# Two transformer blocks in fp32 on one core: weight rings and tiles at multiples of 128 bytes, stationary weights written 72 or 80 bytes further on

## The reference, cut to what matters

```python
# first block
h = rmsnorm(x, attn_norm_w)
proj = h @ w_in                      # attention q, k, v; gated linear attention q, k, v, gate, low-rank codes
x = x + concat([attention, gla]) @ w_out
h = rmsnorm(x, ffn_norm_w)
x = x + (silu(h @ w_gate) * (h @ w_up)) @ w_down
x = rmsnorm(x, final_norm_w)
# second block, modulated by mod = silu(c) @ w_ada + b_ada
h = rms_norm(x, norm_mix) * (1 + sc1) + sh1
x = x + g1 * (hybrid_mixer(h @ w_in_2) @ w_out_2)      # retention, RWKV-7, block-sparse attention
h = rms_norm(x, norm_ffn) * (1 + sc2) + sh2
u = causal_depthwise_conv3(h @ w_ffn_up) + conv_b
x = x + g2 * ((silu(gate) * val) @ w_ffn_down)
out = rms_norm(x, norm_final)
```

## The kernel before, in words

| stage, line | form | matmuls |
|---|---|---|
| mixer 1, L574: q0, k0, q1, k1, gq, gk, 8 units each | columns | 1,152 |
| mixer 1, L574: v0, v1, gv0, gv1, gr0, gr1 (8 units each), out (8 parts of 4) | rows | 576 + 384 |
| mixer 1, L558: codes, 32 weight columns stationary | columns | 48 |
| GLU and conv, each: L574 (2 blocks of 8 units) and L306 (20 blocks) | columns | 384 and 3,840 |
| down 1 and down 2, each: L1762 | rows | 960 |
| down 1 and down 2, each: L1779, the last units, half of them from the ring | rows | 48 + 48 |
| mixer 2, L2084: 9 parts of 8 units | columns | 1,728 |
| mixer 2, L2084 and L2360: 4 parts of 8 units, out (8 parts of 4) | rows | 720 and 48 |

## Time and profile before

### The profile page before, as it was taken

How to read it: one execution, slowest core, us unless ns; L and a number is a source line. 1 busy time by engine, 2 the same in 40 slices (tenths; PEclk the granted TensorE clock), 3 DMA queues, 4 the chain that set the end, 5 groups by cost and what they waited for, 6 DMA issues and landing times.

```text
span 2445.8 us, 43133 instructions
## 1 busy us (share of the span) xinstructions
PE 2425.4 (99%) x18001; PEld 2205.9 (90%) x18001; DVE 1621.5 (66%) x1962; ACT 1149.9 (47%) x1516; POOL 0.3 (0%) x5
## 2 busy tenths in 40 slices
PE   9999999999999999999999999999999999999998
PEld 8889778999999998888899898988999999998886
DVE  5568457777777766777777455566878756664456
ACT  5465344534334334444664344445544444554444
POOL 0000000000000000000000000000000000000000
PEclk9999999999999999999999999999999999999999
DMA  8555467778777766888476344455677655555553
GB/s 280 171 170 182 150 225 268 268 263 289 275 265 285 272 238 251 317 312 293 154 279 242 125 142 139 139 185 195 245 271 258 224 207 189 190 203 193 188 187 121
DMA packets 214566, 541.27 MB, mean 221 GB/s; under 512 B 9130, under 2 KB 15860, under 8 KB 202516
## 3 DMA queue, kind: packets, MB, share of 16 engines
q1 hardware_dynamic: 214420, 539.18, 63.0%
HBM read 533.86 MB, written 5.28 MB: 220 GB/s over the span
## 4 chain that ended last, share of the span: by engine, by line
PE 97%; DVE 1%; ACT 1%; DMA 0%; issue 0%; SPq 0%; DVEq 0%; ACTq 0%
PE ps L306 36%; PE ps L1762 18%; PE ps L574 18%; PE ps L2084 15%; PE ps L1779 2%; PE ps L2602 0%; DMA raw_weights<-in_w_in_dram 0%; PE ps L2360 0%; PE ps L2621 0%; PE ps L974 0%; PE ps L1004 0%; PE ps L432 0%; PE ps L2616 0%; PE ps L986 0%; PE ps L1016 0%
## 5 line engine op out<-in xcount | busy, mean ns | idle before, releaser
L272 DVE TENSOR_TENSOR weights_lo<-raw_weights,weights_hi 128x1024 fp32r<-128x1024 f32 x786 | 957.9, 1224 | 745.4 <-ACT weights_hi L265 741.5
L265 ACT ACTIVATE weights_hi<-raw_weights 128x1024 fp32r<-128x1024 f32 x782 | 827.0, 1061 | 1182.0 <-PE ps L306 459.2
L485 DVE SCALAR_TENSOR_TENSOR ada_acc<-ada_w,col,ada_acc 128x1024 f32<-128x1024 f32 x180 | 230.1, 1278 | 0.1
L306 PE MATMUL ps<-glu_x_hi,weights_hi 128*128 128x256 f32 x1280 | 202.8, 280 | 0.0
L306 PE MATMUL ps<-glu_x_lo,weights_hi 128*128 128x256 f32 x1280 | 202.5, 279 | 0.0
L306 PE MATMUL ps<-glu_x_hi,weights_lo 128*128 128x256 f32 x1280 | 202.5, 279 | 0.0
L306 PE MATMUL ps<-conv_x_hi,weights_hi 128*128 128x256 f32 x1280 | 198.8, 277 | 0.0
L306 PE MATMUL ps<-conv_x_hi,weights_lo 128*128 128x256 f32 x1280 | 197.9, 277 | 0.0
L306 PE MATMUL ps<-conv_x_lo,weights_hi 128*128 128x256 f32 x1280 | 197.9, 277 | 0.0
L306 PEld LDWEIGHTS ps<-glu_x_lo,weights_hi 128*128 128x128 f32 x1280 | 173.2, 188 | 0.0
L306 PEld LDWEIGHTS ps<-glu_x_hi,weights_hi 128*128 128x128 f32 x1280 | 173.1, 188 | 0.0
(11 more groups left out here) (531 smaller groups left out, 3688.2 us busy)
## 6 DMA issues: line engine op xcount, KB each, us to landing
raw_weights<-in_w_in_dram SPq DMA_DIRECT2D x99, 1024.0 KB, 5.3
ada_w<-in_w_ada_dram SPq DMA_DIRECT2D x96, 1024.0 KB, 6.9
raw_weights<-in_w_ffn_up_dram SPq DMA_DIRECT2D x88, 1024.0 KB, 5.3
raw_weights<-in_w_gate_dram SPq DMA_DIRECT2D x44, 1024.0 KB, 5.1
raw_weights<-in_w_up_dram SPq DMA_DIRECT2D x44, 1024.0 KB, 5.1
raw_weights<-in_w_down_dram SPq DMA_DIRECT2D x44, 1024.0 KB, 5.4
raw_weights<-in_w_ffn_down_dram SPq DMA_DIRECT2D x44, 1024.0 KB, 4.8
raw_weights<-in_w_out_dram SPq DMA_DIRECT2D x32, 1024.0 KB, 5.1
```

What stands on the lines that cost most here:

```text
L265: kit.nc.scalar.activation(kit.w_hi_t[:, n % SPLITS, :], raw, ACT.Copy).then_inc(kit.w_hi, 1)
L272: kit.nc.vector.tensor_tensor(kit.w_lo_t[:, n % SPLITS, :], raw, kit.w_hi_t[:, n % SPLITS, :].bitcast(F32), ALU.subtract).then_inc(kit.w_l ...
L306: ins = nc.tensor.matmul(out, lhsT=lhsT, rhs=rhs, start=start and m == 0, stop=(k == KT - 1 and m == 2), skip_group_check=True)
L485: step = nc.vector.scalar_tensor_tensor(acc, w, c, acc, ALU.mult, ALU.add)
```

## The change

1. `weights_hi` and `weights_lo` get 32 values (128 bytes) more in each of the four slots, so a slot starts 4,224 bytes after the one before instead of 4,096, still at a multiple of 128.
2. `base` is rounded up to a multiple of 128 instead of 32. The rings have grown by 1,024 bytes, so it goes from 110,784 to 111,872 = 874 x 128: all tiles that stood at 64 modulo 128 now stand at 0.
3. `Kit.move` records ranges of units that are written further on in their slot: 80 bytes for the columns parts of mixer 1 and for the GLU, 72 bytes for the columns parts of mixer 2 and for conv. The rows parts and both down stages stay at the slot's start. `Kit.slots` gives a unit's two places, and the splits and the matmuls use it instead of `w_hi_t[:, n % SPLITS, :]`. (The codes part is moved too.)

Modulo 128, before and after: columns form, weights at 0 and x at 64, then weights at 80 or 72 and x at 0. Rows form, x at 64 and weights at 0, then both at 0. The last four units of a down stage: x and weights both at 64, then both at 0. The number, order, shape and waits of all instructions and transfers stay.

```diff
@@
+LINE = 128
+MOVED = {"m1": 80, "glu": 80, "m2": 72, "conv": 72}
@@ class Kit
-        self.w_hi_t = sb("weights_hi", [P, SPLITS, UNIT], dt=R32)
-        self.w_lo_t = sb("weights_lo", [P, SPLITS, UNIT], dt=R32)
+        self.w_hi_t = sb("weights_hi", [P, SPLITS, UNIT + LINE // 4], dt=R32)
+        self.w_lo_t = sb("weights_lo", [P, SPLITS, UNIT + LINE // 4], dt=R32)
+        self.moved = []
@@
+    def move(self, first, units, stage):
+
+        self.moved.append((first, first + units, MOVED[stage] // 4))
+
+    def slots(self, n, i=0):
+
+        u = n + 16 * i if isinstance(i, int) else n
+        at = sum(by for a, b, by in self.moved if a <= u < b)
+        return tuple(w[:, n % SPLITS, at:at + UNIT] for w in (self.w_hi_t, self.w_lo_t))
+
@@ split_hi
-    kit.nc.scalar.activation(kit.w_hi_t[:, n % SPLITS, :], raw, ACT.Copy).then_inc(kit.w_hi, 1)
+    kit.nc.scalar.activation(kit.slots(n, i)[0], raw, ACT.Copy).then_inc(kit.w_hi, 1)
@@ split_lo
-    kit.nc.vector.tensor_tensor(kit.w_lo_t[:, n % SPLITS, :], raw, kit.w_hi_t[:, n % SPLITS, :].bitcast(F32),
-                                ALU.subtract).then_inc(kit.w_lo, 1)
+    hi, lo = kit.slots(n, i)
+    kit.nc.vector.tensor_tensor(lo, raw, hi.bitcast(F32), ALU.subtract).then_inc(kit.w_lo, 1)
@@ multiply_block, and in the same way multiply_part, multiply_tiles, Down.tensor, Down.slot, last_units
-        s = n % SPLITS
+        w_hi, w_lo = kit.slots(n, i)
...
-                        wh, wl = (w[:, s, a + c0:a + c1] for w in (kit.w_hi_t, kit.w_lo_t))
+                        wh, wl = (w[:, a + c0:a + c1] for w in (w_hi, w_lo))
@@ FirstMixer
+            if p.form != "rows":
+                kit.move(n, p.units, "m1")
@@ Glu
+        kit.move(self.first, 16 * self.turns, "glu")
@@ SecondMixer
+            if p.form != "rows":
+                kit.move(self.first + n, p.units, "m2")
@@ ConvGlu
+        kit.move(self.first, 16 * self.turns, "conv")
@@ program
-        base = -(-nc.sbuf_base // 32) * 32
+        base = -(-nc.sbuf_base // LINE) * LINE
```

More of the change, by code:

```diff
@@ L294, in multiply_block @@
                         out = kit.ps[:, 2 * j + q, :]
-                        wh, wl = (w[:, s, a:a + UN] for w in (kit.w_hi_t, kit.w_lo_t))
+                        wh, wl = (w[:, a:a + UN] for w in (w_hi, w_lo))
                         h, l = (x[:, k, q * P:(q + 1) * P] for x in (xh, xl))
@@ L542, in multiply_part @@
 def multiply_part(kit, pe, part, n, u, x_hi, x_lo, begun=None):
-    nc, j, s = kit.nc, part.j, n % SPLITS
+    nc, j = kit.nc, part.j
+    w_hi, w_lo = kit.slots(n)
     per = UNIT // part.width
@@ L554, in multiply_part @@
         if part.form == "codes":
-            wh, wl = (w[:, s, a + P - 2 * GRANK:a + P] for w in (kit.w_hi_t, kit.w_lo_t))
+            wh, wl = (w[:, a + P - 2 * GRANK:a + P] for w in (w_hi, w_lo))
             h, l = x_hi[:, k, :], x_lo[:, k, :]
@@ L569, in multiply_part @@
                 out = kit.ps[:, 2 * j + q // 2, (q % 2) * S:(q % 2 + 1) * S]
-                wh, wl = (w[:, s, a + q * P:a + (q + 1) * P] for w in (kit.w_hi_t, kit.w_lo_t))
+                wh, wl = (w[:, a + q * P:a + (q + 1) * P] for w in (w_hi, w_lo))
                 h, l = x_hi[:, k, :], x_lo[:, k, :]
@@ L871, in half_hi @@
         act.wait_ge(self.s_whalf[c], 16)
-        self.kit.nc.scalar.activation(self.kit.w_hi_t[:, 2 * c, :], raw_half(self.kit, 2 * c), ACT.Copy
+        self.kit.nc.scalar.activation(self.kit.slots(2 * c)[0], raw_half(self.kit, 2 * c), ACT.Copy
                                       ).then_inc(self.kit.w_hi, 1)
@@ L1759, in unit @@
                     for q in range(2):
-                        wh, wl = (x[:, s, q * UN:(q + 1) * UN] for x in (kit.w_hi_t, kit.w_lo_t))
+                        wh, wl = (x[:, q * UN:(q + 1) * UN] for x in (w_hi, w_lo))
                         lhsT, rhs = ((h, wh), (h, wl), (l, wh))[m]
@@ L1800, in slot @@
             return tuple(w[:, x, :] for w in self.ext)
-        s = (self.first + p) % SPLITS
-        return self.kit.w_hi_t[:, s, :], self.kit.w_lo_t[:, s, :]
+        return self.kit.slots(self.first + p)
     def tail_hi(self, act, p):
@@ L1820, in next_hi @@
         act.wait_ge(kit.weights_used, self.first + 2 * self.w_tiles - 4)
-        kit.nc.scalar.activation(kit.w_hi_t[:, n % SPLITS, :], raw_half(kit, n), ACT.Copy).then_inc(kit.w_hi, 1)
+        kit.nc.scalar.activation(kit.slots(n)[0], raw_half(kit, n), ACT.Copy).then_inc(kit.w_hi, 1)
     def tail_lo(self, dve, p):
@@ L2352, in last_units @@
     def last_units(self, p, u, hi, lo, t):
-        kit, s = self.kit, (self.first + p.start + u) % SPLITS
+        kit = self.kit
+        w_hi, w_lo = kit.slots(self.first + p.start + u)
         for kk in range(2):
-            wh, wl = (w[:, s, kk * UN:(kk + 1) * UN] for w in (kit.w_hi_t, kit.w_lo_t))
+            wh, wl = (w[:, kk * UN:(kk + 1) * UN] for w in (w_hi, w_lo))
             h, l = (x[:, t * P:(t + 1) * P] for x in (hi[kk], lo[kk]))
```

## The result

The changed kernel takes 2454.51 us (median of 4 runs, 2454.23 to 2456.48) against 2443.67 before (2441.71 to 2445.43): ratio 1.0048, interval 1.0033 to 1.0062, 10.8 us slower. I had forecast 2388, and the range ended at 2436. The profiled spans are 2453.0 and 2445.8, so the profiles show 7.2 of these us. A span is 1.6 us shorter than the time of the same execution (2453.0 for 2454.56), so before's profiled execution took about 2447.4 us by estimate, 3.7 above its median; that is the rest.

What follows compares the result with a forecast made beforehand. It took the spacing of TensorE's matmul starts to bound the kernel. Rows form −25.0, columns form −34.1 and mixer waits +3.4 made −55.7 us, from 2443.6 to a forecast of 2388 us, range 2340 to 2436.

Steps and rivals of the forecast that it cites:

- I take the floor: Columns form, all stages: the new distances keep every matmul at 113.3 ns; 7,658 matmuls gain 4.45 ns each, −34.1 us.
- bound (+16): Columns form: +16 us if the new distance puts the other 3,670 matmuls at 117.8 ns.
- 85%: Mixers: share of their 2,880 columns-form matmuls taken to stand at 117.8 ns, 2,450 with something to gain.
- The rows form: Ring matmuls with x stationary: 3,744 go from 233.3 to 226.7 ns, −25.0 us.
- The distance is now that of the down_last units: Rows form: ring and x both at 0 modulo 128 give the 226.7 ns seen at the down stages' ends.
- rival 3: Rows form: period longer than 128 bytes, slots at 0 or 128 by 256; half the gain goes, 2400, chance 0.06.
- 113.3 is a floor: Columns form: 113.3 ns is the least for a 256-column matmul, since 32-column codes loads run no faster.
- The +3.4 us for waits in the mixers: Mixers: 15% of their 22.4 us gain counted as given back to waits for other engines, +3.4 us.
- Writes 72 or 80 bytes on: ScalarE's and VectorE's splits: shifted writes cost 0; 16 us for 786 splits at 20 ns without cover.
- The rule that the prediction set against its rows: TensorE: independent read ports, so addresses could not matter and time stays 2443.6; the rows say 25 us less.
- 2: Columns form: new distance worse, unaligned loads touch more memory; slower from 118.5 ns, 2511 at 124.5, chance 0.14.
- 1: Columns form: ignores 80 or 72, keeps its mix of spacings, 2420, chance 0.17; all at 117.8 ns, 2436, chance 0.07.

Runs made afterwards that it cites:

- The sweep: Columns-form weights at other distances from x modulo 256, a different one per stage, otherwise as e1; six kernels, 2438.59 to 2456.37 us.
- e1: Against the changed kernel: slots 4,352 bytes apart, base 128 past a multiple of 256, no offsets, so distance 0 modulo 256 everywhere; 2464.71 us, ratio 1.0091.
- e2: As e1, but with the change's offsets kept (80 in mixer 1 and GLU, 72 in mixer 2 and conv); 2449.66 us, ratio 1.0026.
- e9: As e1, but columns-form weights at distance 208 in all four stages, rows form at 0; 2429.05 us, ratio 0.9942.
- e14: As e10, but L306's matmuls in GLU and conv load and write 32 of 128 weight columns, GLU at distance 0; 2439.04 us.
- e10: As e1, but columns-form weights at distance 192 (that of the kernel before) in all four stages, rows form at 0; 2437.64 us, ratio 0.9973.

## Why the prediction was wrong

**The step that failed is the columns form's: "I take the floor".** It was −34.1 us in the sum and measured about +20 in the changed kernel: conv +16.3, mixer 2 some +2.7 and mixer 1 +1.0 (start-to-start means 118.1 for 116.6 and 117.7 for 116.9, over 1,728 and 1,152 matmuls), GLU 0. I had no row for 80 or 72, and argued that a shift of a few bytes loosens a lock. The sweep shows the reverse: among the distances tried the 113.3 exists at 64 and 192 alone, before's 192 was one of them, and every other one gives 116.6 or more. A third of the columns matmuls already stood at 113.3, and I priced their loss only as a bound (+16). The 4.45 ns were right as the step between those two spacings. The share of the mixers' matmuls that stood at the upper one was read a little high, at 85%; their steps show 80% and 75%, which changes the term by 1 us.

**The rows form was right in mechanism and sign, wrong in size.** The term was −25.0; it measured about −10.7 (3,744 at 230.4 instead of 233.3). The step at fault is "The distance is now that of the down_last units", modulo 128. The period is 256: rival 3, which the new stride of 4,224 bytes puts on every other slot. With one distance in all slots e1, e2 and e9 show nearly the whole term: 226.9 ns in down 1, and 22 us over all stages, mixers included (mean 227.3).

**The bound "113.3 is a floor"** rested on the codes' short loads; e14 shows that short loads cost nearly as much. As a number it held in every run.

**The +3.4 us for waits in the mixers** was not seen. The two terms as measured make −10.7 + 20 = +9.3, the spans +7.2. The difference has the other sign and lies mostly at the beginning of mixer 2, where the stretch from its first matmuls to the first long piece takes 25.20 us (1191.82 to 1217.02) instead of 26.66 (1196.62 to 1223.28 before); with one profile of each that may be chance.

**What held:** TensorE's spacing bounds the kernel and no other engine's wait took its place. Writes 72 or 80 bytes on cost the splits nothing (ScalarE's mean is 1061 ns before and after).

**The rule that the prediction set against its rows** (the Trainium skill, TensorE: Matmul & The Clock Gate, Part 2, step ①: loading weights takes no read bandwidth from the running matmul) gives no reason why the place of the weights should matter. In the runs it does matter: e1 and e10 differ only in where the weights of the columns form lie, and their GLU pieces take 92.15 and 90.46 us. That it is read bandwidth that is lost is not shown by them.

**Which rival came true:** 3 for the rows form, and for the columns form a mild case of 2, between it and 1: the mean of 118.0 is above today's mean of 116.3 but under the 118.5 from which I had it decide, because I reckoned with the full 25 us of the rows form. With the 10.7 that were there, it decides from 116.3 + 0.9 = 117.2. Only its sign came true. Its mechanism, a start off a 16- or 64-byte boundary, did not: 208 and 224 are off a 64-byte boundary and at 116.7, 212 is off a 16-byte boundary as well and at 117.3, while 0 and 128 are on both and at 120.0 and 118.7.

**Open:** what the two reads meet in. The table is not smooth, steps of 4 bytes matter, and one set of addresses can hold two spacings. What picks one at a restart was not isolated. Each kernel has one trace, so that the pick repeats from run to run is not shown either: e10's nine runs lie within 3.7 us, and one piece of 768 that changed would be 3.4. Nor is it shown whether the load itself or something else of the stationary operand collides, as a quarter of the load changes so little. Each distance was tried in one or two stages, and the rows form at 0, 128 and 192 only.

## What to carry to other kernels

Where TensorE is busy all the time, read the start-to-start distance of its matmuls by stage and compare it with the columns at the granted clock: 10% were hidden here under a 99% busy engine (117.8 ns where 256 columns take 106.7). Where stationary and moving operand stand relative to each other modulo 256 bytes is worth up to 9% of a matmul with 256 columns (113.3 to 123.3 ns) and 3% with 512 (226.7 to 233.3), it is free to change, and the best distance differs by form: here 0 of three tried for 512 moving columns with x stationary, 64 for 256 with weights stationary. Padding that rotates the distance through a ring averages good and bad. Sweep it on the chip, one distance per stage in one kernel, look at every stretch and not only at the longest, and don't reason from a neighbouring value: 4 bytes off 64, at 68, the spacing was 118.3.

## What the runs showed of the hardware

- fp32r matmuls with back-to-back loads step by 226.7 (distance 0), 232.4 (128) or 233.3 ns (192) with 512 moving columns, and by 113.3 to 123.3 with 256, at a granted clock of 0.998 or 0.999 in all kernels.
- At distances 64 and 192 the same instructions at the same addresses run at 113.3 or 117.8 ns for hundreds to thousands of matmuls, at 48 at 123.3 or 117.8. In the GLU and in conv they change only at an interruption, such as eight transposes.
- The length of the weight load hardly enters: 32 columns loaded and written instead of 128 changed 120.0 to 117.8 or 120.0, and 117.8 to 116.6.
